# A single-core mLSTM block with adaptive normalisation: the first stage with rows scaled in place, plain transposes, and two blocks' columns made by TensorE

## The reference

```python
c_act = jax.nn.silu(c)
mod = c_act @ ada_w[layer] + ada_b[layer]
sh1, sc1, g1, sh2, sc2, g2 = [m[:, None, :] for m in jnp.split(mod, 6, axis=-1)]
h = rms_norm(x) * (1.0 + sc1) + sh1
y = mlstm_mixer(h, ml_w_in[j], ...)        # begins with h @ w_in
x = x + g1 * y
h = rms_norm(x) * (1.0 + sc2) + sh2
x = x + g2 * swiglu(h, ffn_w_gate_up[layer], ffn_w_down[layer])
return rms_norm(x) * final_norm_w
```

## Time and profile before

| | |
|---|---|
| median of 3 runs | 1093.19 us |
| the profiled execution's own time | 1093.14 us |
| its span, first to last instruction | 1091.2 us |
| TensorE busy | 1075.6 us, 99% of the span |
| VectorE busy | 730.0 us, 67% |
| ScalarE busy | 450.3 us, 41% |
| GpSimd busy | 160.7 us, 15% |
| DMA, mean over the span | 162 GB/s |

### The profile page before, as it was taken

The page is one execution under the profiler, slowest core; times in us unless marked ns, Lnnn a source line. Parts: engine busy times, 40 slices in busy tenths (PEclk is TensorE's granted clock), DMA queues, the critical chain, the costliest instruction groups (busy, mean ns, idle before and its releaser), DMA issues.

```text
span 1091.2 us, 14920 instructions
## 1 busy us (share of the span) xinstructions
PE 1075.6 (99%) x5266; PEld 909.1 (83%) x5266; DVE 730.0 (67%) x1284; ACT 450.3 (41%) x826; POOL 160.7 (15%) x145
## 2 busy tenths in 40 slices
PE   6999999999999999999999999999999999999997
PEld 6899888888888888888888888888888888888886
DVE  6857757577578636888667666766666465844666
ACT  7862322231324316764343343334334325444445
POOL 3732312212326522310000000000000000000000
PEclk9999999999999999999999999999999999999999
DMA  9425532432432523116545535453653879665644
GB/s 379 167 78 172 186 110 87 140 109 65 160 116 61 191 78 123 72 39 203 161 138 191 176 106 194 145 169 130 194 173 108 297 275 396 216 192 193 193 155 155
DMA packets 86970, 177.11 MB, mean 162 GB/s; under 512 B 8152, under 2 KB 31320, under 8 KB 85872
## 3 DMA queue, kind: packets, MB, share of 16 engines
q1 hardware_dynamic: 85984, 174.80, 47.1%
q0 software_dynamic: 480, 1.09, 0.4%
q10 hardware_dynamic: 432, 0.27, 0.1%
HBM read 135.97 MB, written 40.16 MB: 161 GB/s over the span
## 4 chain that ended last, share of the span: by engine, by line
PE 97%; DVE 1%; ACT 1%; issue 0%; DMA 0%; DVEq 0%
PE OP L2280 27%; PE OP L2006 20%; PE O L2280 15%; PE ST L2280 5%; PE DC L2280 5%; PE AD L2280 5%; PE O L2006 4%; PE ST L2006 4%; PE AD L2006 2%; PE DC L2006 2%; PE O L2153 1%; PE O L2169 1%; PE DC L2169 1%; PE ST L2136 1%; PE OP L2080 1%; PE ST L2030 0%
## 5 line engine op out<-in xcount | busy, mean ns | idle before, releaser
L2006 PE MATMUL OP<-wH,hH 128*128 128x512 f32 (+1 forms) x400 | 142.1, 355 | 0.1
L1771 DVE TENSOR_TENSOR dL<-dF,dH 128x1024 fp32r<-128x1024 f32 x77 | 93.0, 1223 | 69.5 <-ACT dH L1164 68.7
L2006 PE MATMUL OP<-wH,hL 128*128 128x512 f32 (+1 forms) x400 | 139.0, 348 | 0.0
L2006 PE MATMUL OP<-wL,hH 128*128 128x512 f32 (+1 forms) x400 | 138.7, 347 | 0.0
L1164 ACT CAST dH<-dF 128x1024 fp32r<-128x1024 f32 x77 | 80.0, 1052 | 90.3 <-DMA dF<-w_units 36.4
L2280 PE MATMUL OP<-tH,wsH 128*128 128x512 f32 x264 | 102.7, 389 | 0.0
L2280 PE MATMUL OP<-tL,wsH 128*128 128x512 f32 x264 | 102.7, 389 | 0.0
L2280 PE MATMUL OP<-tH,wsL 128*128 128x512 f32 x264 | 102.7, 389 | 0.0
L2006 PEld LDWEIGHTS OP<-wH,hL 128*128 128x128 f32 x400 | 75.6, 189 | 9.6
L2006 PEld LDWEIGHTS OP<-wH,hH 128*128 128x128 f32 x400 | 75.7, 189 | 9.0 <-issue 0.4
L2006 PEld LDWEIGHTS OP<-wL,hH 128*128 128x128 f32 x400 | 75.8, 190 | 8.6
(11 more groups left out here) (331 smaller groups left out, 2595.9 us busy)
## 6 DMA issues: line engine op xcount, KB each, us to landing
raw<-w_units SPq DMA_DIRECT2D x76, 512.0 KB, 4.6
dF<-act_mid SPq DMA_DIRECT2D x77, 256.0 KB, 2.7
ada<-ada_rest SPq DMA_DIRECT2D x64, 256.0 KB, 2.9
wst<-w_units SPq DMA_DIRECT2D x44, 256.0 KB, 5.1
down_mid<-wst SPq DMA_DIRECT2D x22, 512.0 KB, 3.2
dF<-down_mid SPq DMA_DIRECT2D x44, 256.0 KB, 3.0
dF<-w_units SPq DMA_DIRECT2D x33, 256.0 KB, 6.2
ada<-ada_first SPq DMA_DIRECT2D x8, 1024.0 KB, 10.0
```

Source lines behind the costliest of these rows:

```text
L1771: nc.vector.tensor_tensor(dL[g][:], dF[g][:], dH[g][:].bitcast(F32), ALU.subtract).then_inc(d_L, 1)
L2006: ins = nc.tensor.matmul(out_ap, lhs[a], rhs[b], start=(n == 0 and i == 0), stop=(last and i == 2))
```

## The change

The factor `rstd` is multiplied into the row itself (`scale_row`, on VectorE, for rows 1 and 3 on GpSimd), and TensorE transposes with its transpose mode against the identity. The columns of blocks 0 and 1 come from TensorE alone: eight one-column products of an `ada0` piece with a column of `cact`, for the scale and again for the shift (`columns_from_weights`); VectorE's `sum1` begins at block 2. TensorE starts with 12 products of ones with ones. Block 0 of the first half is projected between rows 5 and 6; rows 6 and 7 therefore go to the banks ST1 and O1. VectorE copies both banks of rows 0 to 3 and the second bank of the later rows; ScalarE copies the first bank of rows 4 to 7. The loads are reordered: `ada0` tile 0 behind row 3, `raw` piece 0 and the gate weights behind row 4, tile 1 and on behind row 7.

```diff
+BY_PE = 2
+WARM = 12
+X_BY_POOL = (1, 3)
@@ where things go and who scaled a row
+        def xt_bank(t, j):
+            return (ST[1], O[1])[j] if t >= 6 else XT_BANKS[2 * (t % 2) + j]
+        def scaled_row(eng, t):
+            if t in X_BY_POOL:
+                eng.wait_ge(x_scaled, X_BY_POOL.index(t) + 1)
+            else:
+                eng.wait_ge(n_hn, t + 1 - sum(p < t for p in X_BY_POOL))
@@ SyncE
-                if k >= 4:
-                    sp.wait_ge(acc0_ok, N1 * (k - 3))
+                if k >= 4 + BY_PE:
+                    sp.wait_ge(acc0_ok, N1 * (k - 3 - BY_PE))
+                elif k >= 4:
+                    sp.wait_ge(mod1_mm, k - 3)
...
-                if t == 2:
+                if t == 3:
                     ada_first_tile(0)
-                if t == 6:
-                    ada_first_tile(1)
+                if t == 4:
+                    load_unit(0, (0,))
                     sp.dma_start(wg_raw[:], w_gates).then_inc(wg_in, 16)
-            load_unit(0, (0,))
-            for k in range(2, KD):
+            for k in range(1, KD):
                 ada_first_tile(k)
-                if k == 3:
+                if k == 2:
                     load_unit(0, (1,))
@@ GpSimd, ahead of the gate weights
+            for t in X_BY_POOL:
+                pool.wait_ge(n_rstd, t + 1)
+                nc.gpsimd.tensor_scalar(xin[:, t, :], xin[:, t, :], rstd[:, t:t + 1], None,
+                                        ALU.mult).then_inc(x_scaled, 1)
@@ ScalarE
                 square(t, xin[:, t, :])
-                if t >= 2:
-                    evac_xT(t - 2)
                 root(t)
-            act.wait_ge(b1_ok, 1)
-            mod_columns(0)
-            modulate(0, 0)
+                if t == 5:
+                    act.wait_ge(b1_ok, 1)
+                    mod_columns(0)
+                    modulate(0, 0)
+                    evac_xT(4)
+                if t == 6:
+                    evac_xT(5)
             evac_xT(NT - 2)
             evac_xT(NT - 1)
             modulate(0, 1)
@@ VectorE
-                diagonal(t)
-                if t >= 2:
-                    evac_xT(t - 2)
+                if t not in X_BY_POOL:
+                    scale_row(t)
                 if 1 <= t <= 3:
-                    sum1(0, 3 * (t - 1), min(3 * t, KD))
-                if t >= 5:
-                    sum1(1, 2 * (t - 5), 2 * (t - 4))
-            sum1(1, 6)
-            evac_xT(NT - 2)
-            evac_xT(NT - 1)
-            for k in range(2, KD):
+                    evac_xT(t - 1, 0)
+                    evac_xT(t - 1, 1)
+                if t == 4:
+                    evac_xT(3, 0)
+                    evac_xT(3, 1)
+                if t > 4:
+                    evac_xT(t - 1, 1)
+            evac_xT(NT - 1, 1)
+            for k in range(BY_PE, KD):
                 sum1(k)
@@ TensorE
+                def columns_from_weights(k, m):
+                    pe.wait_ge(ada0_in[k], 16)
+                    pe.wait_ge(c_act, 1)
+                    if k:
+                        pe.wait_ge(mod1_ok, 2 * k)
+                    for r in range(KD):
+                        ins = nc.tensor.matmul(DC[:, 2 * k + m:2 * k + m + 1], ada0[:, k, r, m * P:(m + 1) * P],
+                                               cact[:, r:r + 1], start=(r == 0), stop=(r == KD - 1))
+                    if m == 1:
+                        ins.then_inc(mod1_mm, 1)
+                for _ in range(WARM):
+                    nc.tensor.matmul(OP[0][:, 0:P], ones[:], ones[:], start=True, stop=True)
...
+                pe.wait_ge(w_L, 1)
+                pe.wait_ge(xT_ok[0], 6)
+                qk_step(0, 0)
+                row_tiles_of_x(6)
+                columns_from_weights(1, 0)
+                row_tiles_of_x(7)
+                columns_from_weights(1, 1)
+                for j in range(2):
+                    pe.wait_ge(xT_ok[j], NT)
+                qk_step(0, 1)
```

More of the change, by code:

```diff
@@ L1319, in sum1 @@
                         dve.wait_ge(acc0_ok, base + r - 1)
-                        if r == KD - 1 and k >= 2:
+                        if r == KD - 1 and k >= 2 + BY_PE:
                             dve.wait_ge(mod1_mm, k - 1)
@@ L2047, in start, with row_tiles_of_x @@
                 pe.wait_ge(const_ok, 5)
-                for t in range(NT):
-                    pe.wait_ge(n_hn, t + 1)
+                def row_tiles_of_x(t):
+                    scaled_row(pe, t)
                     for j in range(2):
-                        if t >= 2:
-                            pe.wait_ge(xT_ok[j], t - 1)
+                        if t == 6:
+                            pe.wait_ge(xT_ok[1], 6)
+                        elif t >= 2:
+                            pe.wait_ge(xT_ok[j], 7 if t == 7 else t - 1)
@@ L2053, in start @@
                         for k in range(4):
-                            ins = nc.tensor.matmul(XT_BANKS[2 * (t % 2) + j][:, k * P:(k + 1) * P],
-                                                   xin[:, t, (4 * j + k) * P:(4 * j + k + 1) * P], diag[:, t % 2, :],
-                                                   start=True, stop=True)
+                            ins = nc.tensor.transpose(xt_bank(t, j)[:, k * P:(k + 1) * P],
+                                                      xin[:, t, (4 * j + k) * P:(4 * j + k + 1) * P], ident[:])
@@ L2061, in start, with qk_step @@
+                for _ in range(WARM):
+                    nc.tensor.matmul(OP[0][:, 0:P], ones[:], ones[:], start=True, stop=True)
+                for t in range(3):
+                    row_tiles_of_x(t)
+                columns_from_weights(0, 0)
+                row_tiles_of_x(3)
+                columns_from_weights(0, 1)
+                for t in range(4, 6):
+                    row_tiles_of_x(t)
                 pe.wait_ge(wg_L, 1)
                 ws = unit_weights(0, 2 * DK)
-                for k in range(KD):
-                    if k % 4 == 0:
-                        pe.wait_ge(w_L, k // 4 + 1)
-                    if 0 < k < KD - 1:
+                def qk_step(k, half):
+                    pe.wait_ge(m_L, 2 * k + half + 1)
+                    hs = h_cols(half)(k)
+                    last = k == KD - 1
+                    for m in range(2):
+                        ins = three(QK_BANKS[2 * half + m][:], tuple(w[:, k, m * DK:(m + 1) * DK] for w in ws),
+                                    hs, k, k, last)
+                        if last:
+                            ins.then_inc(qk_mm, 1)
+                    for i in range(2):
+                        ins = nc.tensor.matmul(OP[half][:], gate_weights[:, k, :], hs[i], start=(k == 0 and i == 0),
+                                               stop=(last and i == 1))
+                    if last:
+                        ins.then_inc(gates_mm, 1)
@@ new lines, in start @@
+                pe.wait_ge(w_L, 1)
[8 more added lines that the diff above has]
+                qk_step(0, 1)
+                for k in range(1, KD):
+                    if k == 4:
+                        pe.wait_ge(w_L, 2)
+                    if k < KD - 1:
@@ L2067, in start @@
                         mod_columns(k + 1)
                     for half in range(2):
-                        pe.wait_ge(m_L, 2 * k + half + 1)
-                        if k == 0:
-                            pe.wait_ge(xT_ok[half], NT)
-                        hs = h_cols(half)(k)
-                        last = k == KD - 1
-                        for m in range(2):
-                            ins = three(QK_BANKS[2 * half + m][:], tuple(w[:, k, m * DK:(m + 1) * DK] for w in ws),
-                                        hs, k, k, last)
-                            if last:
-                                ins.then_inc(qk_mm, 1)
@@ L2079, in start @@
-                        for i in range(2):
-                            ins = nc.tensor.matmul(OP[half][:], gate_weights[:, k, :], hs[i], start=(k == 0 and i == 0),
-                                                   stop=(last and i == 1))
-                        if last:
-                            ins.then_inc(gates_mm, 1)
+                        qk_step(k, half)
             def qk(h, i):
```

42 lines of the change are left out of this document (18 added, 24 removed).

## The result

The changed kernel takes **1102.55 us** (median of 6 runs, 1101.4 to 1103.73) against 1093.2 us for the kernel before, run beside it (6 runs, 1092.02 to 1093.57). The ratio is 1.0088, with a 95% interval from 1.0078 to 1.0098: 9.4 us slower. The profiled execution was the longest of the six, 1103.73 us, with a span of 1101.9 us.

What follows compares the result with a forecast made beforehand. TensorE bounds the kernel through its start on block 0's second half: 1.0 us later, less a 0.2 us wait, +0.8 us on 1093.14 gives 1093.9 us. Held 1092.5 to 1095.4 for this case; full range 1091.2 to 1099.0.

Steps and rivals of the forecast that it cites:

- What bounds: TensorE's start on block 0's second half decides the time; it moves from 28.67 to 29.7, 1.0 us later.
- GpSimd's row, "I take 1.1": GpSimd's scaling of rows 1 and 3, priced at 1.1 us a row between neighbours of 1.04 and 2.72.
- The level of the clock: TensorE's steps up to the second half, priced at full pace: a row about 0.8 us, a column 1.5.
- rival 2: TensorE at half pace when the first half starts: 4.6 us more up to the second half, 1098.5 us; chance 0.24.
- graver form: TensorE at half pace from row 2 on already: 3.8 us more still, 1102.3 us; within the chance of 0.24.
- deciding sign: Block 0's first projection product at 21.4 with 0.4 us and more between the next ones would show half pace.
- A column from weights, "1.5 us": On TensorE, eight one-column products, 16 records, cost 1.5 us; four columns 5.9 us in place of 0.7.
- The early first half is given back: Block 0's first half starts 5.3 us earlier, at 21.4, but the second half only 8.3 us after it, at 29.7.
- The loads: Arrival times in the new load order, among them row 4 at 12.3 and row 5 at 15.1.
- The early products: TensorE's 12 products of ones take 5.6 us at slow pace, end before 8, hidden in the wait for row 0.
- hand-over to the first half: From the second column's end at 16.7 through ScalarE's and GpSimd's work, block 0's first half is released at 21.4.
- Rival 3: GpSimd's rows take 2.72 us each, so the second half comes 2.6 us later: 1096.5 us; chance 0.12.

Runs made afterwards that it cites:

- experiment 1: The changed kernel with all rows scaled by VectorE, none by GpSimd: 1099.01 us, ratio 1.0054 to the kernel before.
- experiment 4: The changed kernel with each transpose made as an ordinary product with the identity: 1102.94 us in one run.
- experiment 5: The changed kernel with all rows scaled by VectorE and every transpose an ordinary product with the identity: 1101.43 us in one run.
- experiment 7: The changed kernel with rows scaled by VectorE, products of ones in TensorE's waits and 20 early products in place of 12: 1097.18 us (5 runs).
- experiment 2: The changed kernel, GpSimd's rows kept, with 14 ordinary products of ones behind row 0: 1105.25 us in one run.
- experiment 3: The changed kernel with the columns of blocks 0 and 1 summed by VectorE as before the change: 1103.54 us in one run.
- experiment 10: The changed kernel with GpSimd scaling rows 1 and 3 by a product of two tensors, the factor spread over 1024 columns: 1100.31 us in one run.
- experiment 6: The changed kernel with rows scaled by VectorE and ordinary products of ones filling TensorE's waits: 1096.64 us (10 runs, 1094.82 to 1099.68).

## Why the prediction was wrong

- **What bounds.** Right: the start of block 0's second half decides. It moved by 9.7 us; 1.4 us more went into that half at half level, and a few tenths of waits fell away; the spans differ by 10.7.
- **GpSimd's row, "I take 1.1".** The term that opened the error. It measures 3.28, outside both bounds (1.04 and 2.72), because the nearest rows were of other forms. The Trainium skill (GPSIMD Engine Reference, section Engine selection) has operations with one input at about line rate there. The traces don't bear that out for this one: the product with a factor for each partition takes three times as long as the copy of the same width (1.04), and the two-input form is faster (1.89). This put row 1 2.3 us late, and by experiment 1 is worth 3.5 us in all, the clock included.
- **The level of the clock.** The step that failed most. The sum priced every step at full level and left the loss to rival 2 with a chance of 0.24. From row 1's start to the second column's end the forecast had 6.1 us and the trace has 11.75, with no wait in it: three rows at 1.7 and two columns at 3.3 us. At full level the same rows and columns would be 6.0 us (0.87 and 1.71 each), so the half level is 5.7 us here, and 1.4 us more in the second half. Experiments 4 and 5 show the level kept from row 1 to the second half with rows made as products, experiment 7 the level lost with transposes and one-column products though TensorE never waits.
- **Rival 2, right in kind and wrong in place.** It put the half level on the stretch from the first half on (4.6 us) and, in its graver form, on row 2 and what follows (3.8 us more), 1102.3 us. Its deciding sign, 0.4 us and more between the first half's products, did not come: they stand 0.23 us apart, and from 27.8 to 38.0 the clock was full. The half level lay ahead of that stretch, where only the part of 3.8 us came, as 5.7, and behind it. That 1102.3 is close to 1102.55 is luck.
- **What the page had said.** The Trainium skill (TensorE: Matmul & The Clock Gate, section Part 4: PE-mode transpose) has it that in one kernel the full clock doesn't engage for transposes. The traces side with it as a warning: 0.50 with transposes, 1.00 with products. They don't bear it out as a fixed rule, since row 0 (1.09 us) ran at full level, as did rows 6 and 7, and the clock came back at 27.8, in row 5's transposes. I weighed the page by the one kind of transposes that the trace showed, those between dense products, which could not decide it.
- **A column from weights, "1.5 us".** 1.71 at full level (experiment 4: 16 records from 20.64 to 22.35). Three of the four stand on the chain to the second half, 0.6 us. Experiment 7's second half starts at 31.30 in place of 29.7: 1.0 us by the end of the second column (17.74 in place of 16.7; its two columns are 0.4 of that), 0.1 up to the first half (22.54), and 0.5 from there, where the column is 0.2 of it and the rows, 0.87 us in place of 0.79, most of the rest.
- **The early first half is given back.** Right as a mechanism: 29.62 to 38.38 is 8.8 us, forecast 8.3.
- **The loads.** Right to 0.2 us for rows 4 and 5 (12.36 and 15.29 against 12.3 and 15.1).
- **The early products.** Right that they are hidden (2.25 to 7.56). The forecast did not ask whether they hold the level until row 0. With 12 or 14 of them, row 0 ran at full level in the six profiled executions where TensorE had waited 1.14 to 1.84 us for it, and mostly or wholly at half in the four where it had waited 2.13 to 2.39. Row 0 comes between 8.5 and 9.1 in each; it is the early products that end earlier or later, by how soon the clock rises under them.

The sum set right: row 1 +2.3 and half level +5.7 up to the second column, hand-over to the first half +0.3, to the second half +0.5, that half itself +1.4, so 1093.9 + 10.2 = 1104.1 us against 1103.73 in the profiled execution.

Rival 3's mechanism came too, larger than its price. Rivals 2 and 3 had been given as alternatives, but in the profiled execution they were one chain, for GpSimd's wait is where the clock fell first. The case of both at once should have had a chance and a price of its own.

What stays open: at what point the clock is lost in a given execution, and what part the transposes and the one-column products each have in it, since no run has the transposes without waits and without the columns. The times of experiments 2 to 5 and 10 rest on one run each, and one program's runs lie up to 4.9 us apart (experiment 6). The mean clock doesn't explain all of such a spread: the kernel before goes from 1091.5 to 1094.5 us at 0.998 to 1.000, and experiment 7 has 1097.18 us at 0.998.

## What to carry to other kernels

Before taking work off TensorE in a stage that is not dense, ask what the engine's clock will do: halving the work of a row saves nothing if the row then runs at half level, and the one-column products and dense work around it may run at half level too. Products put into waits to hold the level need the same care: sized for full level, they stand in the way when it is lost. Price a form of operation only from rows of that very form; where there is none, the bounds must be wider than the neighbours. And when two risks share a wait, give them one joint price, not two separate ones.

## What the runs showed of the hardware

- GpSimd's product of a 128x1024 float32 tile with a factor for each partition takes 2.85 to 3.37 us (four traces), the same with the factor spread as a second tensor 1.89 us (experiment 10), a copy of that width 1.03 or 1.04 us. VectorE does the first in 0.75 us, and in up to 1.40 us while GpSimd works beside it (experiment 1).
- The granted clock fell to half in waits (at 10.7 in the changed kernel) and also under transposes and one-column products that leave TensorE no wait at all (at 17.4 in experiment 7), and stayed at half from 14 to 26 in the changed kernel with TensorE's records filling every window. In experiment 6 the same program takes 1094.8 to 1099.7 us; a mean clock of 0.997 against 0.993 is all that the summary shows of it.
- Eight 128x128 transposes of float32 take 0.8 to 0.9 us at full level and 1.7 at half, where eight ordinary products take 1.8 and 3.5. Eight one-column products take 1.7 and 3.3.
